# Grouping the head steps of three attention stages two to a place, and scaling rows ahead of plain transposes

## What is computed

```python
# first block: 8 sparse heads, 8 stick-breaking heads
score = einsum(relu(q_idx @ k_idx), w_idx)          # 8 index heads
idx = top_k(where(causal, score, -inf), 64)         # keys that each token may see
sparse: softmax(q k / 8 + bias[t - s]) over idx, times v
stick:  u = log_sigmoid(-z);  a = exp(log_sigmoid(z) + sum of u between s and t);  a @ v
o = concat(rmsnorm(oa), rmsnorm(ob)) @ w_out
# second block, layer 0: differential attention
a = softmax(q0 k0) - lam * softmax(q1 k1)
o = rms_norm(a @ v, subln_g) * (1 - lambda_init);   h = h + o @ w_o
# second block, layer 1: latent attention
s = (q_nope k_nope + q_rope k_rope) * 192 ** -0.5
o = softmax(causal(s)) @ v;                         h = h + o @ w_o
```

## Time and profile before

| what | us |
|---|---|
| median of 3 runs | 1249.62 (1249.36 to 1252.39) |
| the profiled execution, its own time | 1246.54 |
| its span, first to last instruction | 1245.2 |
| TensorE busy | 1172.4 |
| VectorE busy | 807.0 |
| ScalarE busy | 615.2 |

### The profile page before, as it was taken

One profiled execution on the slowest core, in us unless ns is written; L12 is line 12 of the kernel. 1 busy time (PEld: TensorE's weight loads), 2 busy tenths in 40 slices (PEclk: granted clock), 3 DMA queues, 4 the chain that ended last, 5 costly groups with the idle time before them and its releaser, 6 DMA issues.

```text
span 1245.2 us, 19659 instructions
## 1 busy us (share of the span) xinstructions
PE 1172.4 (94%) x7782; PEld 1079.5 (87%) x7782; DVE 807.0 (65%) x1343; ACT 615.2 (49%) x1096; POOL 57.0 (5%) x75
## 2 busy tenths in 40 slices
PE   1899999999897999999999888999999999999998
PEld 1799989899886999999988777999998888899997
DVE  6888878657654665665567776655566765665554
ACT  4444444645554644444554445545546544545453
POOL 4000000000000000000001110000000100000000
PEclk8899999999898999999999999999999999999999
DMA  9999888353221366655342213555553514455540
GB/s 382 351 401 362 328 307 311 116 203 134 73 99 68 112 244 213 225 207 201 136 173 103 99 72 117 188 195 179 200 173 133 203 69 152 169 175 198 179 160 34
DMA packets 34011, 231.78 MB, mean 186 GB/s; under 512 B 3704, under 2 KB 5120, under 8 KB 6528
## 3 DMA queue, kind: packets, MB, share of 16 engines
q1 hardware_dynamic: 31952, 226.24, 49.8%
q10 hardware_dynamic: 1968, 4.29, 1.0%
HBM read 229.45 MB, written 1.06 MB: 185 GB/s over the span
## 4 chain that ended last, share of the span: by engine, by line
PE 82%; DVE 11%; ACT 4%; issue 1%; POOL 1%; DMA 1%; DVEq 0%; SPq 0%; ACTq 0%; POOLq 0%
PE ps L374 39%; PE pacc L374 35%; DVE wlo L337 2%; ACT wk L974 2%; PE ps L384 2%; DVE raw L315 1%; PE ps L387 1%; PE pacc L384 1%; POOL st L481 1%; ACT whi L336 1%; DVE st L969 1%; PE pacc L387 1%; PE pacc L513 1%; PE ps L513 1%; DVE tmp L650 1%
## 5 line engine op out<-in xcount | busy, mean ns | idle before, releaser
L337 DVE TENSOR_TENSOR wlo<-raw,whi 128x1024 fp32r<-128x1024 f32 x353 | 430.2, 1224 | 191.4 <-ACT whi L336 186.1
L336 ACT ACTIVATE whi<-raw 128x1024 fp32r<-128x1024 f32 x353 | 368.9, 1054 | 160.0 <-PE pacc L374 88.3
L374 PE MATMUL ps<-nhi,whi 128*128 128x256 f32 x1392 | 404.8, 291 | 19.6 <-DVE wlo L337 17.2
L374 PE MATMUL ps<-nhi,wlo 128*128 128x256 f32 x1392 | 396.1, 285 | 0.0
L374 PE MATMUL ps<-nlo,whi 128*128 128x256 f32 x1392 | 396.0, 285 | 0.0
L374 PEld LDWEIGHTS ps<-nhi,whi 128*128 128x128 f32 x1392 | 269.1, 193 | 26.3 <-ACT whi L336 18.7
L374 PEld LDWEIGHTS ps<-nlo,whi 128*128 128x128 f32 x1392 | 269.1, 193 | 5.1 <-issue 1.0
L374 PEld LDWEIGHTS ps<-nhi,wlo 128*128 128x128 f32 x1392 | 268.9, 193 | 0.0
L374 PE MATMUL pacc<-whi,hhi 128*128 128x512 f32 x444 | 174.9, 394 | 1.1 <-ACT sg L717 1.1
L374 PE MATMUL pacc<-wlo,hhi 128*128 128x512 f32 x444 | 174.0, 392 | 0.0
L374 PE MATMUL pacc<-whi,hlo 128*128 128x512 f32 x444 | 172.8, 389 | 0.0
(11 more groups left out here) (285 smaller groups left out, 1358.3 us busy)
## 6 DMA issues: line engine op xcount, KB each, us to landing
raw<-in_stream SPq DMA_DIRECT2D x213, 1024.0 KB, 4.9
gates<-in_g_post ACTq DMA_DIRECT2D x3, 512.0 KB, 13.7
h<-in_x SPq DMA_DIRECT2D x1, 1024.0 KB, 7.1
cst<-in_const ACTq DMA_DIRECT2D x1, 1024.0 KB, 9.4
arena<-bias_rows ACTq DMA_DIRECT2D x1, 1024.0 KB, 14.4
out<-tmp SPq DMA_DIRECT2D x4, 256.0 KB, 2.1
silu_c<-in_c_row ACTq DMA_DIRECT2D x1, 512.0 KB, 5.8
arena<-in_final_g SPq DMA_DIRECT2D x1, 512.0 KB, 5.8
```

The lines of the kernel that those rows point to most:

```text
L336: t_hi = act.do(lambda e: e.activation(whi[:, s, :], src, ACT.Copy), arrived, room)
L337: t_lo = dve.do(lambda e: e.tensor_tensor(wlo[:, s, :], src, whi[:, s, :].bitcast(F32), ALU.subtract), arrived, room, t_hi)
L374: return e.matmul(o, lt[a], rh[b], start=start and first, stop=stop and last)
```

## The change

`nudge` runs up to two steps where it ran one, and there are half as many places: two in a projection unit, two in an output unit, two in a latent block. The numbers of places that steps wait are about halved, with these exceptions: the eight rounds of the selection follow one another by one place (three before), a sparse head begins three places after the selection was written (at once before), a differential head's step O follows V by four places (four before, so twice as far), and a latent head's T follows S by three places (five before). Two stick projections move ahead of the first sparse ones in `IN_ORDER`. In the differential heads the copy and the two diagonals go, the result is scaled while it is copied, and O is two plain transposes. In the latent heads the diagonals go, the rows of the softmax are scaled in place, and T is three plain transposes.

```diff
-IN_ORDER = [8..11] + (12,0),(16,0),(12,1),(16,1),(0,0),(4,0),(12,2),(16,2), (12,3),(16,3),(0,1),...
+IN_ORDER = [8..11] + (12,0),(16,0),(12,1),(16,1),(12,2),(16,2),(0,0),(4,0), (12,3),(16,3),(0,1),...
 class Side:
-    def __init__(self, width, gap=4):
+    def __init__(self, width, gap=2):
     def nudge(self):
         self.now += 1
-        if self.active and self.active[0][0] <= self.now:
-            self.advance(self.active.pop(0)[1])
-        elif len(self.active) < self.width:
-            self.begin()
+        for _ in range(2):
+            if self.active and self.active[0][0] <= self.now:
+                self.advance(self.active.pop(0)[1])
+            elif len(self.active) >= self.width or not self.begin():
+                return
 def products(...):
-                    if between is not None and k % 2 and k < len(pairs) - 1:
+                    if between is not None and k % 4 == 3 and k < len(pairs) - 1:
                         between()
 def rows_times(...):
                     for o in outs:
                         done[i].append(products([o], after))
-                        if between is not None:
-                            between()
+                    if between is not None:
+                        between()
 index_part:    after two index heads    yield 3 -> yield 2
                after a round            yield 3 -> yield 1
+            sel_at.append(side.now)
 stick_head:    yield 6, yield 6 -> yield 3, yield 3
 ripe:          side.now - born[j] >= 4 -> >= 2
 half_out:      yield 5 -> yield 3
-            side.add(sparse_head(hh), lambda hh=hh: ripe(hh // 2, 4 + hh // 2) and len(t_sel) == 2)
+            side.add(sparse_head(hh), lambda hh=hh: ripe(hh // 2, 4 + hh // 2) and sel_at and side.now >= sel_at[0] + 3)
-            if n == len(IN_ORDER) - 2:
+            if n == len(IN_ORDER) - 1:
                 banks.retire(fix)
 diff_head:     after S   yield 6 -> yield 4
-            t_ov = dve.do(lambda e: e.tensor_copy(ov.ap[:, 0:T], b.ap[:, 0:T]), t, ov.free)
+            for i in range(2):
+                t_ov = dve.do(lambda e: e.tensor_scalar(ov.ap[:, i * P:i * P + P], b.ap[:, i * P:i * P + P],
+                                                        r[:, i:i + 1], None, ALU.mult), t, ov.free)
             banks.give(b, t_ov)
-            for i in range(2):
-                t = dve.do(lambda e: e.tensor_scalar(ds.ap[:, i * P:i * P + P], ident, r[:, i:i + 1], None, ALU.mult),
-                           t, ds.free)
-            yield
+            rooms.give(ds, t)
+            yield 4
             b = banks.take()
             for i in range(2):
-                tk = pe.do(lambda e: e.matmul(b.ap[:, i * P:i * P + P], ov.ap[:, i * P:i * P + P],
-                                              ds.ap[:, i * P:i * P + P], start=True, stop=True), t, t_ov, b.free)
+                tk = pe.do(lambda e: e.transpose(b.ap[:, i * P:i * P + P], ov.ap[:, i * P:i * P + P], ident), t_ov, b.free)
 latent_head:
-            by = [ds.ap[:, i * P:i * P + P] for i in range(2)]
             for i in range(2):
-                t = dve.do(lambda e: e.tensor_scalar(by[i], ident, rs[:, i:i + 1], None, ALU.mult), t, ds.free)
-            yield 5
-            pt, t = transpose_p(ex, [*t_e, t], by)
+                a, w = widths(i)
+                t = dve.do(lambda e: e.tensor_scalar(ex.ap[:, a:a + w], ex.ap[:, a:a + w], rs[:, i:i + 1], None,
+                                                     ALU.mult), t)
+            yield 3
+            pt, t = transpose_p(ex, t)
-        side = Side(5, 3)
+        side = Side(5, 2)
                 products of a uq block:
-                if k < 2:
+                if k == 1:
                     side.nudge()
```

More of the change, by code:

```diff
@@ L23 @@
 OUT_ORDER = (4, 5, 6, 7, 0, 1, 2, 3)
-IN_ORDER = [8, 9, 10, 11] + [g + j for g, j in ((12, 0), (16, 0), (12, 1), (16, 1), (0, 0), (4, 0), (12, 2), (16, 2),
+IN_ORDER = [8, 9, 10, 11] + [g + j for g, j in ((12, 0), (16, 0), (12, 1), (16, 1), (12, 2), (16, 2), (0, 0), (4, 0),
                                                 (12, 3), (16, 3), (0, 1), (4, 1), (0, 2), (4, 2), (0, 3), (4, 3))]
@@ L936, in masked, with transpose_p @@
             put(b.ap[:, 0:3 * P], identr[:, :], mask.rearrange("p n w -> p (n w)"), True, False, b.free, *after)
-        def transpose_p(p, t_p, by=None):
+        def transpose_p(p, t_p):
             b = banks.take()
@@ L943, in transpose_p @@
                 o, a = b.ap[:, n * P:(n + 1) * P], p.ap[:, n * P:(n + 1) * P]
[L944 to L947, removed]
+                tk = pe.do(lambda e: e.transpose(o, a, ident), t_p, b.free)
             rooms.give(p, tk)
@@ L983, in scaled_out @@
             return t
+        sel_at = []
         wi = new_stat(16)
@@ L1010, in index_part @@
                 if hh % 2:
-                    yield 3
+                    yield 2
             best = new_stat(16)
@@ L1017, in index_part @@
                                                         score[:, i, 0:P * (i + 1)], TAKEN), t[i]) for i in range(2)]
-                yield 3
+                yield 1
             for i in range(2):
@@ L1060, in stick_head @@
             t = dve.do(lambda e: e.scalar_tensor_tensor(lg.ap, z, 0.0, lg.ap, ALU.max, ALU.add), t)
-            yield 6
+            yield 3
             b2 = banks.take()
@@ L1118, in ripe @@
         def ripe(*js):
-            return all(j in t_q and side.now - born[j] >= 4 for j in js)
+            return all(j in t_q and side.now - born[j] >= 2 for j in js)
         o1 = Parts(nhi, nlo, {4: (mhi[:, 0, :], mlo[:, 0, :]), 5: (mhi[:, 1, :], mlo[:, 1, :]),
@@ L1293, in diff_head @@
             r, t = rstd(ssq, P, 1e-5, t)
-            t_ov = dve.do(lambda e: e.tensor_copy(ov.ap[:, 0:T], b.ap[:, 0:T]), t, ov.free)
+            for i in range(2):
+                t_ov = dve.do(lambda e: e.tensor_scalar(ov.ap[:, i * P:i * P + P], b.ap[:, i * P:i * P + P], r[:, i:i + 1],
+                                                        None, ALU.mult), t, ov.free)
             banks.give(b, t_ov)
-            for i in range(2):
-                t = dve.do(lambda e: e.tensor_scalar(ds.ap[:, i * P:i * P + P], ident, r[:, i:i + 1], None, ALU.mult),
-                           t, ds.free)
-            yield
+            rooms.give(ds, t)
+            yield 4
             b = banks.take()
             for i in range(2):
-                tk = pe.do(lambda e: e.matmul(b.ap[:, i * P:i * P + P], ov.ap[:, i * P:i * P + P],
-                                              ds.ap[:, i * P:i * P + P], start=True, stop=True), t, t_ov, b.free)
+                tk = pe.do(lambda e: e.transpose(b.ap[:, i * P:i * P + P], ov.ap[:, i * P:i * P + P], ident), t_ov, b.free)
             rooms.give(ov, tk)
-            rooms.give(ds, tk)
             chunk_parts(n2, hh, b, tk, g8, t_g8)
@@ L1418, in latent_head @@
             banks.give(b, *t_e)
-            rs, ds = new_stat(2), rooms.take()
+            rs = new_stat(2)
             t = dve.do(lambda e: e.reciprocal(rs, sm), t_e)
-            by = [ds.ap[:, i * P:i * P + P] for i in range(2)]
             for i in range(2):
-                t = dve.do(lambda e: e.tensor_scalar(by[i], ident, rs[:, i:i + 1], None, ALU.mult), t, ds.free)
-            yield 5
-            pt, t = transpose_p(ex, [*t_e, t], by)
-            rooms.give(ds, pe.last())
+                a, w = widths(i)
+                t = dve.do(lambda e: e.tensor_scalar(ex.ap[:, a:a + w], ex.ap[:, a:a + w], rs[:, i:i + 1], None,
+                                                     ALU.mult), t)
+            yield 3
+            pt, t = transpose_p(ex, t)
             yield
```

## The result

The changed kernel takes 1232.95 us (median of 4 runs, 1232.68 to 1236.05) where the kernel before takes 1249.49 (median of 4): a ratio of 0.9873, with a 95% interval of 0.9845 to 0.9901, 16.5 us by the medians. The profiled execution fell from 1246.5 to 1232.7, 13.9 us. The forecast was 1232.

The account below looks back on a forecast made before the run. TensorE, busy 94% of the span, was taken as the bound, with VectorE second. Terms -6.0 - 1.5 + 2.2 + 1.1 - 11.7 - 1.0 = -16.9 us gave a 1232 us median; range 1224 to 1241, with rivals 1221 to 1245.

Parts of the forecast that it names:

- largest term: Differential heads: VectorE needs 11.2 us a head, TensorE runs ahead until a step stops it; -11.7 us.
- 2.6 for a lag: Differential stage: VectorE may lag 2.6 us behind TensorE before the transposes of the softmax stop it, taken up once.
- the last wait: Last of seven waits for step O's diagonals, in the output units where VectorE has less to do; 2.5 us saved.
- Rival 1: Differential stage: TensorE alone sets it, giving 18.6 us there; total -27, 1222 us; chance 0.13.
- Rival 2: All three stages: waits only move and the clock falls as often; about -1 us, 1248; chance 0.15.
- The next stop: Differential heads: TensorE's next stop is at T, four places behind S, some 7.5 us of TensorE's time.
- Selection: First sparse head: the 3.1 us wait for the selection and the clock's fall behind it go; -6.0 us.
- Start of the output: Last projection to output product: norm begun half a unit sooner, ahead of the split; -1.5 us, between 0 and -3.
- The term of 2.2 for parts just ahead of their use: Output units: transposes of chunks 5 and 0 come just before their reader, 1.1 us each in full view; +2.2.
- Latent stage: Latent heads: cheaper T gives -3.4 us, new waits between S and T +2.4; together -1.0, between -5 and +4.
- Rival 3: Latent stage: plain transposes let the clock fall, three stretches costing 8.7 us; total -8, 1241; chance 0.07.
- Rival 4: Heads of three stages: clock falls at every head's T, kernel slower; twelve extra falls give 1267 us; chance 0.05.

Follow-up runs that it names:

- the arithmetic alone: Kernel before with rows scaled and plain transposes in differential and latent heads, all places and steps as they were: 0.9923 of the kernel before.
- the second execution of the changed kernel: The changed kernel with nothing altered, timed once more beside the kernel before: 1233.22 us against 1247.59, ratio 0.9888.
- the run without it: Changed kernel with the old order of stick and sparse projections, sparse heads begun as soon as the selection is written: 0.9926 of the kernel before.
- the old latent places: Changed kernel with the latent stage's places and yields as before and its new arithmetic: 0.9866 of the kernel before.

## Why the prediction was right, and where it was not

**Right in its largest term.** VectorE's least cycle was put at 11.2 us, from 11.8 less 0.2 less 0.4. Measured: 11.0 to 11.1, in the changed kernel and in the one with the arithmetic alone, and it stayed so when a head was begun later. The differential stage was forecast at -11.7 + 1.1 = -10.6 us and gave -11.8. From the first head's softmax to the last it was 84.3 us before and is 75.1 now. Of the four parts of the -11.7, two can be held against rows: the cycles gave 6 by 0.7 = 4.2 where 3.6 was put, the clock up to 3.4 where 3.0 was. The other two, 2.6 for a lag and 2.5 for the last wait, no run separates. Rival 1 (TensorE alone, 9.7 us a head) is out: a stop of up to 1.4 us stands in six cycles, for what VectorE has yet to do. Rival 2 (the waits only move, -3.6) is out too: some did move, but 13.2 us of them became 5.8. But the 0.80 of GpSimd's power, which I said can't go, can: it goes when the waiting instruction is issued later.

**The next stop was named wrongly.** I let TensorE run ahead until T and counted 2.6 us of lag. It stops at the scores, one step earlier in the cycle, for keys that VectorE has yet to rotate; I had costed the chain behind the scores and not the one ahead of them. The 2.6 also took 4.9 us for S on VectorE, where its own figures give 4.7 and the trace 4.8 (691.34 to the end of the last L1281 at 696.18). The lag taken up once was thus worked out for the wrong step, and that the stage's sum held in spite of it is luck as far as that term goes; the cycle carries the rest.

**Selection: right size, wrong reason.** -6.0 us was forecast, and no stop and no lower clock is left there. From the stage's start to its last projection product TensorE took 138.0 us before and 132.0 in the second execution of the changed kernel, each with a stretch of 3.4 us at 0.50 ahead of the heads. I gave the distance as the reason; the run without it shows that the dense rounds suffice.

**Start of the output: mis-sized.** -1.5 was forecast, measured is -0.3 in the interval (12.2 to 11.8), in both executions. I had the norm begin 1.4 us sooner, and it did by 1.25; but I took the split that stood ahead of it to be out of the way, and it moved to a place behind the norm and still ahead of the parts. The term of 2.2 for parts just ahead of their use was right: 1.2 us each, and 1.2 for the last differential chunk. Behind the first output product the stage grew by less than the 2.2, 1.2 us in the second execution, where less of the lower clock fell on it than before. Together the first stage was forecast at -5.3 and gave -5.8 and -5.2 in two executions, of which the second had a stretch of 3.4 us at 0.50 (at 271.6) ahead of the heads, as the kernel before did, and the first had none.

**Latent stage: the step that failed.** -1.0 was forecast, +2.3 came: TensorE's waits in the stage grew from 5.5 to 8.3 us, and its busy time fell by 0.5. I counted only the wait between S and T. The one that matters is ahead of S. `ripe` asks four old places, which at three to a block were 1.33 blocks; two new ones, at two to a block, are one block, 0.33 less, some 0.4 us of products, and TensorE waits for the copy of the queries. One place more removes 4.1 us. I had read `ripe` as halved with everything else. Also T was put at 0.42 us less a head; from start to start T's matmuls take 5.2 us in the stage before and 2.4 with the arithmetic alone, 0.35 a head and 2.8 in all, where 3.4 was put, and of this the stage shows only 1.0.

**The clock.** Rival 3 did not come: 1.00 from 975 to 1022 with plain transposes. The Trainium skill ("TensorE: Matmul & The Clock Gate", Part 4) has it that transposes do not count as activity as matmuls do; no run here shows a fall that can be laid to them alone. In one execution of the kernel with the old latent places the clock fell in that stage, at 1006.9, in a stop of 1.70 us ahead of a T; with the arithmetic alone the same stop, 1.69 us, was followed by no fall. Its figure of some 275 ns for one, given there for bf16, agrees with how long each is recorded here (0.27 us in the median), but it is not what they cost in a row: three take 0.24 us here, since they overlap. Rival 4 is out too, since no head's stop in the changed kernel's differential or latent stage was followed by the lower clock.

**That the sum met the median** to 1 us is partly luck: -16.9 was forecast, -16.5 came by the medians of the first timing, -14.4 by those of the second, and -13.9 by the profiled executions. The latent stage's miss of 3.3 us was made up by the differential stage's 1.2 and by the kernel before having a median 2 to 3 us higher in the first timing (1249.49) than in the later ones (1246.63 to 1247.59).

## What to carry to other kernels

Before stretching a wait, count how much of the second engine's queue a cycle fills, its own waits inside a chain with it: here 11.0 us of an 11.8 us cycle, so a stop of 1.8 us gave back 0.8 a head, and the rest only once and by the clock. An instruction that is moved in a queue, as the split ahead of the norm was, has left a chain only if it now stands behind the chain's last instruction. When places are thinned out, convert every distance into the work between its ends, one by one; a number that is halved is not the same distance in each loop. Work moved to a freer engine must not wait there at the head of a queue that others need.

## What was not expected of the hardware

The lower clock followed stops of about 2 us in some heads and not in others: two stretches of 3.4 us in the differential stage before, behind stops of 1.85 and 1.76 us, and none behind the longest of its seven, 2.54 us; none with the arithmetic alone (seven stops, the longest 2.2 us). At the start of the first block's output product it was at 0.50 for 10.2 us before and for 13.7 and 6.8 us in two executions of the changed kernel. Yet from the last projection product to the first output product both took 11.8 us: TensorE's slower work only shortened its wait for VectorE, from 3.67 to 2.79 us. The lower clock costs time only where TensorE has no wait to fill, here 0.8 us behind the first output product (32.9 us to the stage's end in place of 32.0).

An instruction that waits costs what stands behind it in its queue. The Trainium skill ("TensorE: Matmul & The Clock Gate", table at its head) says that ScalarE and VectorE work strictly in order; the trace agrees: ScalarE's 4.05 us for GpSimd held up a split of 1.07 us and with it VectorE, 1.96 us.
